# Expert weights in 2 MB transfers with 16 KB rows and ten staged slots, with the GpSimd copies gated by GpSimd itself

## The reference, cut to what matters

```
logits = x2 @ w_router + b_router
top_vals, top_idx = top_k(logits, 4);  gates = softmax(top_vals)
for each block of rows that belong to expert e:
    gu = xb @ w_up[e] + b_up[e]                    # w_up[e]: 1024 x 2048
    gate, up = min(gu[:, :1024], 7), clip(gu[:, 1024:], -7, 7)
    act = (up + 1) * (gate * sigmoid(1.702 * gate))
    out = act @ w_down[e] + b_down[e]              # w_down[e]: 1024 x 1024
y[token] += gate_weight * out
```

## Time and profile before

| | us |
|---|---|
| median of 3 runs | 1289.42 |
| lowest, highest | 1287.0, 1290.28 |
| span of the profiled execution, first to last instruction | 1288.5 |
| TensorE busy in it | 1174.2 |
| GpSimd busy in it | 467.4 |

### The profile page before, as it was taken

One profiled execution on the slowest core, in us unless ns is written; L12 is line 12 of the kernel. 1 busy time (PEld: TensorE's weight loads), 2 busy tenths in 40 slices (PEclk: granted clock), 3 DMA queues, 4 the chain that ended last, 5 costly groups with the idle time before them and its releaser, 6 DMA issues.

```text
span 1288.5 us, 30593 instructions
## 1 busy us (share of the span) xinstructions
PE 1174.2 (91%) x11113; PEld 577.5 (45%) x11114; DVE 605.2 (47%) x1256; ACT 249.7 (19%) x487; POOL 467.4 (36%) x833
## 2 busy tenths in 40 slices
PE   8999999999999899798979998989989799899876
PEld 7777777775434333233323433433333233233232
DVE  2999983122644344354343442444524244444243
ACT  2012124001222122122212221212211122122112
POOL 1022300000444435445451454454444444535451
PEclk9999999999999999999989999999999999999997
DMA  9983442344899999999998799999999999999996
GB/s 260 337 269 119 144 135 105 129 155 166 334 385 399 421 421 422 421 421 421 422 421 364 307 398 422 420 422 421 422 421 421 421 421 421 422 421 408 421 421 254
DMA packets 94570, 448.97 MB, mean 348 GB/s; under 512 B 8526, under 2 KB 42894, under 8 KB 45339
## 3 DMA queue, kind: packets, MB, share of 16 engines
q1 hardware_dynamic: 93742, 446.55, 86.5%
q10 hardware_dynamic: 749, 1.19, 0.3%
q0 software_dynamic: 48, 0.85, 0.2%
HBM read 447.00 MB, written 2.42 MB: 349 GB/s over the span
## 4 chain that ended last, share of the span: by engine, by line
PE 55%; DMA 15%; DVE 13%; POOL 6%; issue 6%; SPq 3%; ACT 1%; DVEq 0%; POOLq 0%; ACTq 0%
PE banks L1369 20%; DMA ring<-in_w_down 15%; PE banks L1379 12%; DVE R L800 8%; PE banks L1164 8%; POOL ring L530 6%; PE banks L1086 4%; PE banks L1144 3%; PE banks L1123 2%; PE banks L1280 2%; SPq L398 1%; PE banks L1130 1%; PE banks L1153 1%; DVE R L809 1%; DVE R L812 0%
## 5 line engine op out<-in xcount | busy, mean ns | idle before, releaser
L1369 PE MATMUL banks<-ring,hT 128*32 128x512 f32 x3328 | 430.4, 611 | 62.3 <-POOL ring L530 57.5
L530 POOL COPY ring<-big 128x512 f32<-128x512 f32 x248 | 146.9, 641 | 554.4 <-SPq L404 554.4
L530 POOL COPY ring<-R 128x512 f32<-128x512 f32 x496 | 289.9, 631 | 113.4 <-DMA R<-in_w_up 113.4
L321 DVE TENSOR_TENSOR xt<-xt,banks 128x1024 f32<-128x1024 f32 x106 | 128.7, 1215 | 403.7 <-PE banks L1144 403.7
L1379 PE MATMUL banks<-ring,hT 128*32 128x256 f32 x3328 | 227.4, 392 | 18.4 <-DMA ring<-in_w_down 13.2
L1379 PEld LDWEIGHTS banks<-ring,hT 128*32 128x32 f32 x3328 | 107.5, 113 | 202.8 <-issue 123.3
L1164 PE MATMUL banks<-hT,ring 128*128 128x288 f32 x768 | 189.2, 407 | 0.2 <-ACT hT L554 0.2
L1369 PEld LDWEIGHTS banks<-ring,hT 128*32 128x32 f32 x3328 | 95.5, 111 | 195.6 <-POOL ring L530 81.1
L1164 PEld LDWEIGHTS banks<-hT,ring 128*128 128x128 f32 x768 | 145.7, 191 | 39.9 <-issue 0.3
L680 ACT COPY WT<-banks 128x256 f32<-128x256 f32 x52 | 19.4, 373 | 498.2 <-PE banks L1379 498.2
L800 DVE SCALAR_TENSOR_TENSOR R<-big,convw,R 128x256 f32<-128x256 f32 x240 | 108.1, 525 | 0.0
(11 more groups left out here) (252 smaller groups left out, 757.2 us busy)
## 6 DMA issues: line engine op xcount, KB each, us to landing
ring<-in_w_down SPq DMA_DIRECT2D x128, 1024.0 KB, 11.0
R<-in_w_up SPq DMA_DIRECT2D x124, 1024.0 KB, 18.1
ring<-in_w_up SPq DMA_DIRECT2D x70, 1024.0 KB, 9.4
big<-in_w_up SPq DMA_DIRECT2D x62, 1024.0 KB, 12.7
ring<-in_w_in SPq DMA_DIRECT2D x24, 1024.0 KB, 10.3
ring<-in_w_branch_b SPq DMA_DIRECT2D x4, 1024.0 KB, 4.9
ring<-in_w_branch_a SPq DMA_DIRECT2D x4, 1024.0 KB, 4.9
ring<-in_w_out SPq DMA_DIRECT2D x4, 1024.0 KB, 4.9
```

The lines of the kernel that those rows point to most:

```text
L321: nc.vector.tensor_tensor(dst, dst, rows, ALU.add).then_inc(y_added, 1)
L530: ins = nc.gpsimd.tensor_copy(ring[:, k, h * 512:(h + 1) * 512], parked[k][:, h * 512:(h + 1) * 512])
L1369: ins = mm(UP[g * BLK:(g + 1) * BLK, :], xT[:, k, :], ring[:, k, g * 512:(g + 1) * 512], start=k == 0, stop=k == UP_SLOTS - 1)
```

## The change

Expert weights are now handled in units of two slots (2 MB, 128 partitions x 16 KB): units 0 to 3 are w_up, units 4 and 5 w_down. Partition q of unit u holds rows 256u+2q and 256u+2q+1 of w_up, or four rows of w_down, so a partition's 16 KB are contiguous in HBM. Five units (0 to 4, ten slots) of the next expert are staged in one area `staging` of 10 MB, and only unit 5 (the second half of w_down) goes straight into the ring. The mixing stage's tensors now lie inside `staging`.

SP no longer waits for `up_used`. For each place p it issues staged units 0, 1, 2 of p+1 (each when both GpSimd copies of that unit of p are done), then unit 5 of p after the fourth `down_used`, then staged units 3 and 4 of p+1. GpSimd runs a loop over the places: it reads `items_before`, and waits itself for `staged_full` and `up_used` or `down_used`; it copies ten slots per place, two copies of 1024 columns each. The semaphore `slot_free` is counted and awaited by no one.

Also: `turn_rows` takes every second column, `turn_raw` and the turn of b_up every fourth; one small load (`ffn_rows`) and a ninth row group in `cols` are added; the store of old state rows moves from GpSimd's queue to ACT's; the loads of `norm_final_g` move from ACT, before the experts, to SP, behind the last expert load, into ring slot 0; the scratch for GpSimd's own transfers is cut.

```diff
-            for k in range(UP_SLOTS):
-                sp.wait_ge(*mix_block_used(MIX_BLOCKS - SLOTS + k))
-                load_slot(0, k)
+            for u in range(UP_UNITS):
+                sp.wait_ge(*mix_block_used(MIX_BLOCKS - SLOTS + 2 * u + 1))
+                load_unit(0, u)
             sp.wait_ge(ya_evac, 2 * KC)
-            for k in range(PARKED - 1):
-                load_parked(1, k)
-            for k in range(UP_SLOTS, SLOTS):
-                sp.wait_ge(*mix_block_used(MIX_BLOCKS - SLOTS + k))
-                load_slot(0, k)
-            load_parked(1, PARKED - 1)
+            for u in range(UP_UNITS):
+                load_staged(1, u)
+            sp.wait_ge(*mix_block_used(MIX_BLOCKS - 1))
+            for u in range(UP_UNITS, UNITS):
+                load_unit(0, u)
+            load_staged(1, STAGED - 1)
             sp.wait_ge(before_known, 1)
             with sp.Fori(1, NE - 1) as place:
...
-                release_parked(before)
-                load_up_rest(here, before)
-                load_parked_again(place + 1, after, range(0, 2))
-                load_down(here, before)
-                load_parked_again(place + 1, after, range(2, PARKED))
+                load_staged_again(place, after, range(AHEAD))
+                load_last_unit(here, before)
+                load_staged_again(place, after, range(AHEAD, STAGED))
...
-            for e in range(1, NE):
-                for k in range(PARKED):
-                    pool.wait_ge(parked_full[k], 16 * e)
-                    pool.wait_ge(released, (e - 1) * PARKED + k + 1)
-                    for h in range(4):
-                        ins = nc.gpsimd.tensor_copy(ring[:, k, h * 512:(h + 1) * 512], parked[k][:, h * 512:(h + 1) * 512])
-                    ins.then_inc(slot_full[k], 16)
+            def copy_slot(u, h):
+
+                for c in range(2):
+                    lo = h * SLOT + c * (SLOT // 2)
+                    ins = nc.gpsimd.tensor_copy(ring[:, 2 * u + h, c * (SLOT // 2):(c + 1) * (SLOT // 2)],
+                                                staged[u][:, lo:lo + SLOT // 2])
+                ins.then_inc(unit_full[u], 8)
+
+            pool.wait_ge(before_known, 1)
+            with pool.Fori(1, NE) as place:
+                before = pool.value_load(items_before[0:1, bass.ds(place - 1, 1)], min_val=0, max_val=MAX_ITEMS)
+                for u in range(UP_UNITS):
+                    pool.wait_ge(staged_full[u], place * 16)
+                    pool.sem_inc(slot_free, 1)
+                    for h in range(2):
+                        pool.wait_ge(up_used, before * UP_SLOTS + (2 * u + h + 1))
+                        pool.sem_inc(slot_free, 1)
+                        copy_slot(u, h)
...
-                pairs = raw.rearrange("t (b p h) -> t b h p", h=2, p=P)
+                fours = raw.rearrange("t (p c) -> t c p", c=4)
                 for c in range(4):
-                    ins = tr(TB[:, c * P:(c + 1) * P], pairs[:, c // 2, c % 2])
+                    ins = tr(TB[:, c * P:(c + 1) * P], fours[:, c])
```

More of the change, by code:

```diff
@@ L136, in hybrid_layer, with part @@
         first_place = sb("first_place", [NE, 1])
[L138 to L142, removed]
+        staging = sb("staging", [P, STAGED, UNIT])
+        staged = [staging[:, u, :] for u in range(STAGED)]
+        early = staging[:, 0:UP_UNITS, :].rearrange("p u n -> p (u n)")
+        taken = [0]
+        def part(n, rows=P):
+            lo = taken[0]
+            taken[0] = lo + n
+            assert taken[0] <= UP_UNITS * UNIT
+            return early[0:rows, lo:lo + n]
+        big, R1, R2, R4 = part(KC * CB), part(KC * T), part(KC * T), part(KC * T)
+        R3 = staging[:, STAGED - 1, 0:KC * T]
+        spb = part(G * P).rearrange("p (g i) -> p g i", g=G)
+        tmpc = part(2 * T).rearrange("p (c t) -> p c t", c=2)
+        glu_tail = part(KC * NS).rearrange("p (c t) -> p c t", c=KC)
+        convw = part(KC * W).rearrange("p (c k) -> p c k", c=KC)
+        vecrows = part(P, 8 * KC)
+        WS = part(G * NS, NS).rearrange("p (g i) -> p g i", g=G)
+        mean_w = part(P)
+        ffn_rows = part(256, QN)
+        xs_rows = spb[0:NS].rearrange("p g i -> p (g i)")
         def view(t, c):
-            return t[:, :].rearrange("p (c t) -> p c t", c=c)
+            return t.rearrange("p (c t) -> p c t", c=c)
         convbuf = view(big, KC)
@@ L381, in _ @@
                 load_block(n)
[L383 to L393, removed]
@@ new lines, in load_unit, with load_staged, load_staged_again @@
+            def load_unit(e, u):
+                sp.dma_start(ring[:, 2 * u:2 * u + 2, :].rearrange("p s n -> p (s n)"), unit_source(e, u)
+                             ).then_inc(unit_full[u], 16)
+            def load_staged(e, u):
+                sp.dma_start(staged[u], unit_source(e, u)).then_inc(staged_full[u], 16)
+            def load_staged_again(place, after, us):
+                for u in us:
+                    sp.wait_ge(unit_full[u], place * 16 + 16)
+                    load_staged(after, u)
@@ L1363, in _, with up @@
             keep_busy(2)
-            def up(k, fills):
-                pe.wait_ge(slot_full[k], fills)
+            def up(k, half, full):
+                pe.wait_ge(unit_full[k // 2], (half, full)[k % 2])
                 for g in range(4):
@@ L1371, in up, with down @@
                 ins.then_inc(up_used, 1)
-            def down(j, fills):
-                pe.wait_ge(slot_full[UP_SLOTS + j], fills)
+            def down(j, half, full):
+                if j < 3:
+                    pe.wait_ge(unit_full[UP_UNITS + j // 2], half if j == 0 else full)
                 for h in range(2):
@@ L1448, in _ @@
                         combine(0, row_out[0])
-            last = (pe.value_load(items[0:1, bass.ds(bodies, 1)], min_val=0, max_val=COLUMN_MAX) & (NE - 1)) * 16 \
-                + 16 * (FILLS + 1)
+            last = (pe.value_load(items[0:1, bass.ds(bodies, 1)], min_val=0, max_val=COLUMN_MAX) & (NE - 1)) * 16
             turn_raw(bodies)
```

116 lines of the change are left out of this document (56 added, 60 removed).

## The result

| | before | after |
|---|---|---|
| median, us | 1289.43 | 1294.21 |
| lowest, highest (6 runs each) | 1287.0, 1290.28 | 1292.94, 1297.34 |
| span of the profiled execution | 1288.5 | 1292.6 |
| VectorE busy | 605.2 | 667.3 |
| GpSimd busy | 467.4 | 649.2 |

What follows compares the result with a forecast made beforehand. The prediction took the DMA stream of expert weights as the bound. Start 9.0, rate 11.6, three-item place 0 and tail -3.4 summed to 17.2 us less, 1272 us, range 1258 to 1290.

Steps and rivals of the forecast that it cites:

- The rate: Expert weight stream: 16 KB runs raise 421 to 427.4 GB/s, 2.453 us per MB instead of 2.49, a gain of 11.6 us.
- The prediction's line: DMA cost per run, drawn through 1 KB and 8 KB runs: 9.4 ns fixed and 37.7 ns per KB.
- The start: Stream up to 465.1 us: more staged bytes fill early gaps, a lead of 3.6 MB, worth 9.0 us.
- the forecast's last gap: First places, before 465.1 us: engines lose about 2 us once more until a w_down step releases the direct unit.
- The steady stretch: Remaining 314 MB at 0.037 us less each, 11.6 us, if SP's new order never empties the queue.
- some 4 us to spare: Steady stretch, two-item places: next direct unit released near 45 us, while units already issued keep the engines until 49.
- The place with three items: Single place in the stream: engines idle 11.0 and 3.4 us, sum 14.4 as before, so nothing gained.
- The tail: From data end to span end: 19.1 us instead of 15.7, a loss of 3.4.
- 2.3 us per slot: GpSimd's copies of staged slots: same time as before, 23 us of copies per 29.4 us place.
- SP's in-order wait empties the queue: Rival at two-item places: about 2.8 us per slot makes some 17 places lose about 1.1 each; 1291 us, chance 0.09.
- The sum: Whole kernel: data end 1252.1 plus tail 19.1 is span 1271.2; median 0.9 above, 1272 us, chance 0.46.
- lead: Weights in by 465.1 us beyond those of before: 3.6 MB, worth 9.0 us.

Runs made afterwards that it cites:

- e3: Changed kernel with its 2 MB transfers kept but each partition's 16 KB laid out as two runs of 8 KB: 1297.86 us, 1.0068 of the changed kernel.
- e7: Changed kernel with only the first of two 1024-column GpSimd copies per staged slot, so half of each is left out: 1280.41 us, 0.9932 of the changed kernel.
- e10: Changed kernel with only the direct w_down unit cut into two 1 MB halves, each issued after its own w_down step: 1273.87 us, 0.9872 of the changed kernel.
- e4: Changed kernel with GpSimd's copies four times 512 columns per slot instead of twice 1024: 1374.15 us, 1.0652 of the changed kernel.

## Why the prediction was wrong

**The rate: right.** Full windows at 427 to 430 GB/s against 427.4; e3 shows that it is the run. At 2.439 us per MB it gave 4 us more than forecast. (The prediction's line gives 408.8 GB/s for 4 KB, not 408.6; nothing hangs on it.)

**The start: right in its sum, partly by luck.** By 465 us 69.2 MB were in, forecast 69.5. But the direct units of the first places were issued 2 to 4 us later than forecast (355.96, 388.75 and 421.46 against 354.0, 385.7 and 417.2), VectorE being held, and the forecast's last gap, near 450, did not come: the place there has one item, not the two that were assumed.

**The steady stretch: here it failed.** The forecast: "TensorE is held, but the queue has some 4 us to spare", and "TensorE's bodies" at 15.8 us. Measured: 26 us idle in gaps, where 1.1 was forecast. Three errors in one step:
- It followed one place from a full queue and found 4 us to spare. The queue is fed over three places (items 2, 2, 1). At each of two places with two items TensorE needs 31.7 us for 29.3 of data, so the spare goes. Over the five bodies of a turn TensorE has 79 us of work for 87.8 us of data and could catch up, but once in the turn it is made to wait for the direct unit. What it loses there it never gets back. Followed over 91 us, as above, the same rows show it.
- It took the body after the wait at full clock. The granted clock fell to 0.50 during the wait: 2.3 us each time.
- It took 15.8 for every body. Held VectorE adds 1.06 us to the turn, and all copies' second halves together are worth 13.8 us (e7). A row for it was there: the earlier trace rows has GpSimd busy for 43 of 100 us, and the forecast itself put it at 23 of 29.4.

Without the last two the turn would be 91.0 - 2.3 - 1.1 = 87.6 us, just under 87.8; the margin was far below the 4 us of the text.

**The place with three items: the mechanism right, the size off.** 17.0 us idle against 14.4, in two pieces as forecast (12.2 and 4.8 against 11.0 and 3.4).

**The tail: too long.** Data ended at 1275 + 5 x 220/430 = 1277.6, the span at 1292.6: 15.0, forecast 19.1. The data end now has the 0.6 MB of `norm_final_g` in it; from the last weights it is 16.5. No engine shows a wait for these loads, so they cost nothing beyond, as forecast.

**GpSimd: too slow in the forecast.** 2.3 us per slot were assumed, 16.10 us for eight slots are 2.0. So the rival "SP's in-order wait empties the queue" had nearly the right time (1291), but not the cause: GpSimd kept up, and the gaps were some ten of 1 to 4 us and not 17 of 1.1.

**The sum.** Data end of the weights 1276.1 against 1252.1, 24.0 later: idle time +27.9, rate -4.4, lead +0.7 make 24.2. The tail is 2.6 shorter on the same count, and the median stands 1.6 above the span instead of 0.9. 24.0 - 2.6 + 0.7 is 22.1, and measured are 22.2 (1294.2 - 1272.0). With the loop mended by one edit (e10) the kernel takes 1273.9.

## What to carry to other kernels

When a buffer's refill waits for the engine and the engine waits for that refill, walk the chain once around until it closes, over as many items as its pattern has, and compare the turn with the time of its bytes; a margin worked out for one step from a full queue says nothing. Large transfers are good for the rate, but the one that an engine waits for should be issued and awaited in pieces as small as the step that uses it. Before giving GpSimd more copies, look at which VectorE instructions between SBUF operands run beside them and who waits for those.

## What the runs showed of the hardware

- Back-to-back GpSimd copies of 512 columns held one VectorE `tensor_scalar` (L1037 of e4) until the whole row of copies had ended (median 3.95 us, longest 6.15, 0.29 when free), while others (L770) got in after one copy. With 1024 columns all but one hold of this step in after were about one copy long. What decides between the two is not shown.
- Of a full queue with 128 partitions: 348 GB/s with 1 KB runs, 421 with 8 KB, 427 to 430 with 16 KB. Transfers of 2 MB with 8 KB runs gave 422 to 423.
- TensorE's granted clock fell to 0.50 during a wait of 5.9 us and cost 2.3 us after it; it also fell to 0.50 in a wait of 4.7 us (e10), and through one of 2.5 us it stayed at 1.00.
